# Another order of the units in a grouped-query attention, and the wait of its output projection

## The chip, the cores and the metric

The kernel runs on one core of a Trainium2 chip. The metric is the device time of one execution in microseconds; the kernel before was timed three times (median 2070.47, from 2069.06 to 2070.81). The engines are PE (TensorE), DVE (VectorE), ACT (ScalarE), POOL (GpSimd) and SP (which here only issues transfers); each works through its own instructions in order, and they wait for each other by semaphores.

## What is computed

The whole reference is a chain: a first block (differential attention, neighbourhood attention, a mixture of experts, a gated side input) and then two layers over 512 tokens and a context of 256 rows, all in float32 with a model width of 1024. The first of these two layers holds the grouped-query attention that the change touches. Its 16 query heads of 64 columns share 4 key and value heads. Queries of the 512 tokens see 768 keys (256 of the context, 512 of the tokens); queries of the context see only the context's 256 keys. Both results are gated and go through the same output projection:

```
o  = gqa_attend(q,  concat(kc, k), concat(vc, v))     # 512 rows, 768 keys
y  = (o * silu(g)) @ w_out
qc = rms_norm(proj_c[..., q columns])
oc = gqa_attend(qc, kc, vc)                           # 256 rows, 256 keys
yc = (oc * silu(gc)) @ w_out
```

`gqa_attend` is scores times head_dim ** -0.5, a softmax in float32 and the product with the values. `y` and `yc`, scaled by a gate, are added to the residual, and the second of the two layers (a latent attention, MLA) starts from a norm of that.

## The kernel before, in words

Rows are worked on in tiles of 128: tiles 0 to 3 are the tokens, 4 and 5 the context (`XT` = 4, `AT` = 6). Everything here stands in `second_layers` (L1607); both attentions of this part of the kernel are made by the class `Attention` (L233), which writes out the instruction streams of PE (`tensor`, L294), DVE (`vector`, L429), ACT (`scalar`, L499) and POOL (`gpsimd`, L418).

The work of the grouped-query attention is a list of units, built in L1763. A unit is one pair of heads `p` (eight pairs) and one query tile `t`: for `t` of 0 to 3 over all six key tiles (a token unit), for `t` of 4 and 5 over key tiles 4 and 5 (a context unit). Six units make a pair, four for tokens and then two for the context, so there are 48. The fifth entry of a unit is its output group: the token units of pair `p` are group `2p`, its context units group `2p + 1`. `out_of` (L1767) says where a group's result goes: `gT_x[:, p]` for the tokens, `gT_c[:, p]` for the context, both preloaded with silu of the gate.

For each unit PE makes the scores of both heads into four PSUM banks (L324; there is one such area, so the scores of unit n+1 wait until the exponentials of unit n have read it), DVE finds the negated row maxima (L440), and ACT makes the exponentials with their row sums (L515). PE transposes the weights in pieces of four tiles (L336: three pieces for a token unit, one for a context unit), and the pieces are copied to SBUF by ACT (the first of a unit) and DVE (the others), both through the helper line L205. PE then multiplies them with the values (L350). When the last unit of a group is through, DVE takes the reciprocals of the sums (L496), POOL spreads them over the head's columns (L427), PE transposes them (L370), and DVE multiplies gate, sum and reciprocal in two steps (L472, L477).

PE's order in step n is written out in L379 to L393: scores of unit n+1; the turn, if one is due; the weights of unit n; the values of unit n-1; and the reciprocals' transposes if unit n-1 closed a group. DVE's order (L482 to L497) is: the maxima of unit n+1, its pieces of the turn, its pieces of the weights of unit n, and the closing. ACT's (L521 to L527) is: its pieces of the turn, its piece of the weights, the exponentials of unit n+1.

A turn is the transposition of the next pair's queries (and, for pairs 0, 2, 4 and 6, of the next key head) from rows to columns (`gqa_turn`, L1750; PE in L309). It has two pieces of 4 and 2 tiles for the queries and, on an even pair, two more of 4 and 2 tiles for the keys, which are copied twice. The first and third piece are DVE's, the second and fourth ACT's. A turn is due two steps before the first unit of its pair (`turn_step`, L250), that is in the step of the fifth unit of the pair before. Turn pieces, weight pieces and reciprocals go through one ring of three PSUM banks: a piece is written when the piece three before it has been emptied (`take`, L298 to L303).

Behind the attention PE starts the output projection (L1908 to L1943): for both context tiles and both halves of the output columns, four products of eight matmuls of 512 columns each (L1847), whose first seven steps need the groups of pairs 0 to 6 and whose last needs pair 7. Then follow the tokens' tiles, and the norm and the products of the next layer in an order written out in `low_order` (L1684). SP issues the next layer's first weights once the last value product is counted (L1801). The projection adds its result to the residual in L2242 and L2244.

Of the kernel before, what the change touches and what calls it, by code (L numbers as in the profile page):

```python
# [19 lines left out]
DK = D // P  # L20
GRID_W, ROWS, CB = 64, 8, 16
SEQ, CTX = 512, 256
XT, CT = SEQ // P, CTX // P
AT = XT + CT
# [182 lines left out]
def view(t, at, *dims):  # L207

    v = t[:, at:at + math.prod(dims)]
    if len(dims) == 1:  # L210
        return v
    axes = "abcd"[:len(dims)]
    return v.rearrange(f"p ({' '.join(axes)}) -> p {' '.join(axes)}", **dict(zip(axes, dims)))
# [19 lines left out]
class Attention:  # L233
# [56 lines left out]
    def slot(self, n):  # L290
        og = self.units[n][4]
        return og % 2, n - self.members[og][0]
# [1314 lines left out]
def second_layers(nc, c, m, A, base, side_w, extra, arena, ring_in, mods, tabs_2, l1_tabs, ys):  # L1607
# [4 lines left out]
    TT = (4, 5, 0, 1, 2, 3)  # L1612
    at6 = XT * D + CT * D + XT * 96 + XT * 32 + 2 * AT * 32 + 64
    (tc, tsn, tk, _), ((gain_0, shift_0, gate_0), (gain_1, shift_1, gate_1)) = l1_tabs, mods


# [4 lines left out]
    gT_x, gT_c = view(arena, 21504, DK, SEQ), view(arena, 25600, DK, CTX)  # L1621
# [128 lines left out]
    def gqa_turn(p):  # L1750
        q_of = [proj[:, t, 512 + p * P:512 + (p + 1) * P] for t in range(AT)]
        k_of = [proj[:, t, (p // 2) * 64:(p // 2 + 1) * 64] for t in range(AT)]
        pieces = [(q_of[a:e], P, [qT[:, p % 2, a * P:e * P]]) for a, e in ((0, 4), (4, AT))]
        if p % 2 == 0:
            pieces += [(k_of[a:e], 64, [kT[64 * x:64 * x + 64, p // 2 % 2, a * P:e * P] for x in range(2)]) for a, e in ((0, 4), (4, AT))]
        return pieces

    def gqa_ready(pe):
        pe.wait_ge(s["normed"], 18)
        pe.wait_ge(s["ev_act"], units.by[unit["g", DK - 1]][1] + 1)  # L1760
    gqa = Attention(nc, m, sem_of("gqa_"), dict(S=S, T=T, O=O, pr=view(arena, 27648, 2, 2, AT * P), pT=view(arena, 8192, 2, 2 * AT, P), nm=nm, sm=sm, rc=rc, ratio=None,
                                                wide=view(side_w, 3072, 2, 4, 2, 64)),
                    [(p, t, 0, AT, 2 * p, t) if t < XT else (p, t, XT, AT, 2 * p + 1, t - XT) for p in range(8) for t in range(AT)], 2, 1,  # L1763
                    [gqa_turn(p) for p in range(8)],
                    2, lambda p, x, t, lo, hi: (qT[64 * x:64 * x + 64, p % 2, t * P:(t + 1) * P], kT[64 * x:64 * x + 64, p // 2 % 2, lo * P:hi * P]),
                    lambda p, x, kt: proj[:, kt, 256 + (p // 2) * 64:256 + (p // 2 + 1) * 64], 64,
                    lambda og: gT_c[:, og // 2] if og % 2 else gT_x[:, og // 2], gate=True, ready=dict(ring=gqa_ready))  # L1767

    q1T, k1T = view(arena, 8192, 2, 2, SEQ), view(side_w, 0, 2, 2, AT * P)

# [21 lines left out]
    with nc.Block() as block:  # L1792
# [39 lines left out]
        def _(pe):  # L1832
            done = [0]

            def start(key):

                u = unit[key]
                assert u == done[0], key
                done[0] += 1
                if u >= 4:  # L1840
                    act, k = units.by[u - 4]
                    pe.wait_ge(s["ev_act"] if act else s["ev_dve"], k + 1)
                return ps[:, u % 4]

            def product(out, lhs, rhs, ks, K=DK):
                for k in ks:
                    last = pe.matmul(out, lhs(k), rhs(k), start=(k == 0), stop=(k == K - 1))  # L1847
                return last
# [9 lines left out]
            weights_of = lambda i: (lambda k: slot(i + k // 4)[:, k % 4])  # L1858
# [53 lines left out]
            gated = lambda t: (lambda k: gT_x[:, k, t * P:(t + 1) * P]) if t < XT else (lambda k: gT_c[:, k, (t - XT) * P:(t - XT + 1) * P])  # L1912
            first = {(t, cc): start(("o", t, cc)) for t in (4, 5) for cc in range(2)}
            for (t, cc), out in first.items():
                product(out, gated(t), weights_of(2 * cc), range(DK - 1))
            pe.wait_ge(s["gqa_emptied_act"], gqa.emptied[1])
            pe.wait_ge(s["gqa_emptied_dve"], gqa.emptied[0])
            for (t, cc), out in first.items():
                product(out, gated(t), weights_of(2 * cc), (DK - 1,)).then_inc(s["mm"], 1)
            seen_norms = 0  # L1920
            arrived_1 = lambda i, n: pe.wait_ge(s["weights_in"][i], 16 * n)
            for what, t in low_order[2:]:
# [38 lines left out]
            first = {(t, cc): start(("z", t, cc)) for t in (0, 1) for cc in range(2)}  # L1961
# [428 lines left out]
def build(nc, A, prm_at, const_at, stop=None, dbg=None):  # L2390
    with ExitStack() as top:
        def sb(c, name, shape, dt=F32):
            return c.enter_context(nc.sbuf_tensor(name, shape, dt))

        prm = sb(top, "params", [P, sum(n for _, n in prm_at.values())])
        cst = sb(top, "consts", [P, sum(n for _, n in const_at.values())])
        m = {k: prm[:, a:a + n] for k, (a, n) in prm_at.items()}
        m.update({k: cst[:, a:a + n] for k, (a, n) in const_at.items()})


        words = [XT * D, CT * D, XT * 96, XT * 32, 2 * AT * 32, 64, 4 * AT * 64, AT * DK, AT * DK, 2 * D, AT * DK, AT * DK, D]
        base = sb(top, "residual", [P, sum(words)])
        at = lambda n: sum(words[:n])
        hx = view(base, 0, AT, D)
        tc, tsn, tk = view(base, at(2), XT, 96), view(base, at(3), XT, 32), view(base, at(4), 2, AT, 32)
        tkn, tabs_2 = view(base, at(5), 1, 64), view(base, at(6), 4, AT, 64)
        mods = [[view(base, at(7), AT, DK), view(base, at(8), AT, DK), view(base, at(9), 2, D)],
                [view(base, at(10), AT, DK), view(base, at(11), AT, DK), view(base, at(12), 1, D)]]
        rows = lambda v: v.rearrange("(t p) d -> p t d", p=P)

        side_w = sb(top, "side", [P, XT * D])
        extra, arena = sb(top, "extra", [P, 2112]), sb(top, "arena", [P, 30720])
        with semaphores(nc, "ahead", ring_in=6) as ahead:
            with ExitStack() as c:
                ys = first_layer(nc, c, m, A, prm, cst, const_at, base, side_w, extra, arena, ahead["ring_in"], mods, tabs_2, (tc, tsn, tk, tkn))
            with ExitStack() as c:
                second_layers(nc, c, m, A, base, side_w, extra, arena, ahead["ring_in"], mods, tabs_2, (tc, tsn, tk, tkn), ys)
# [34 lines left out]
```

## Time and profile before

| | |
|---|---|
| median of 3 runs | 2070.47 us (2069.06 to 2070.81) |
| the profiled execution: its time, its span | 2071.58 us, 2069.8 us |
| mean granted TensorE clock | 0.958 of full speed |
| PE busy | 1811.1 us, 88% of the span |
| PE weight loads | 1016.0 us, 49% |
| DVE busy | 734.1 us, 35% |
| ACT busy | 521.6 us, 25% |
| POOL busy | 150.3 us, 7% |
| chain that ended last, by engine | PE 31%, issue 17%, DVE 2%, ACT 2%, POOL 1% |

Times in the rows are counted from the span's start. "Busy" is a share of the span. In a timeline a row is a run of like instructions: start, length, engine, line, operation, output and inputs, how many, and in brackets how long the engine had been idle before it and what it had waited for. Matmuls are pipelined, so that the length of a row of them reaches a little into the next one; the distance of two starts is what counts. The grouped-query attention runs from 1262 to 1487 us, the latent attention from 1782 on. The granted clock (PEclk) is the share of full speed that the chip's throttle gave TensorE in a stretch: 1.00 is 2.4 GHz, and the lower level is half of it.

### The profile page before, as it was taken

The page shows a single profiled execution, that of the slowest core. Times are in us where ns is not written, and L with a number is a line of the kernel's source. Part 1 is how long each engine was busy: PE and PEld are TensorE (multiplying, and loading weights), DVE is VectorE, ACT ScalarE, POOL GpSimd, SP SyncE. Part 2 cuts the span into 40 slices and gives each one's busy share as a digit, 9 for nine tenths or more (in the row PEclk, how much of TensorE's full clock was granted, in tenths as well). Part 3 has the DMA queues.
Part 4 walks back from the last instruction along what each step waited for, and adds up shares of the span by engine and source line. Part 5 has one row for each costly group of instructions (what it writes and reads, how often), then busy time and mean ns, then how long its engine had stood idle before and what let it go on. Part 6 is the DMA issues. An engine that isn't in the chain of part 4 may idle for free.

```text
span 2069.8 us, 24033 instructions
## 1 busy us (share of the span) xinstructions
PE 1811.1 (88%) x9628; PEld 1016.0 (49%) x9628; DVE 734.1 (35%) x1431; ACT 521.6 (25%) x1102; POOL 150.3 (7%) x201
## 2 busy tenths in 40 slices
PE   7999878978887778784999998888998999699998
PEld 3333455544444444442464444666644544466663
DVE  2333576231131110120213264666424225455542
ACT  2111476210000001110223123444311233234330
POOL 1110000001111111100000130000000000100000
PEclk9999899999999999997999999999999999899999
DMA  7554937369999999996432220000200011000001
GB/s 246 205 195 166 182 54 119 115 264 387 420 420 420 421 420 421 418 421 262 176 109 81 81 81 1 1 1 2 90 6 31 21 56 61 21 1 1 1 22 41
DMA packets 91871, 333.18 MB, mean 161 GB/s; under 512 B 10096, under 2 KB 26608, under 8 KB 64752
## 3 DMA queue, kind: packets, MB, share of 16 engines
q1 hardware_dynamic: 81536, 310.56, 41.2%
q0 software_dynamic: 5120, 16.78, 2.0%
q10 hardware_dynamic: 5104, 4.30, 0.7%
q8 instruction: 77, 1.26, 0.3%
q14 instruction: 34, 0.28, 0.0%
HBM read 317.32 MB, written 14.30 MB: 160 GB/s over the span
## 4 chain that ended last, share of the span: by engine, by line
PE 31%; issue 17%; DVE 2%; ACT 2%; POOL 1%; POOLq 0%; ACTq 0%; DVEq 0%
PE tail_ps L1847 27%; PE tail_ps L324 2%; ACT arena L515 1%; PE tail_ps L1855 1%; PE tail_ps L336 1%; POOL side L427 1%; POOL extra L2384 1%; PE tail_ps L350 0%; DVE arena L2343 0%; PE tail_ps L309 0%; DVE side L205 0%; DVE tail_small L440 0%; DVE arena L2344 0%; PE tail_ps L370 0%; DVE residual L2244 0%
## 5 line engine op out<-in xcount | busy, mean ns | idle before, releaser
L987 PE MATMUL mix_ps<-arena 128*64 128x256 f32 x2048 | 258.9, 410 | 88.9 <-issue 60.3
L987 PEld LDWEIGHTS mix_ps<-arena 128*64 128x64 f32 x2048 | 165.4, 148 | 181.6 <-issue 90.2
L1847 PE MATMUL tail_ps<-arena 128*128 128x512 f32 x504 | 219.7, 592 | 0.0
L440 DVE TENSOR_REDUCE tail_small<-tail_ps 128x1 f32<-128x768 f32 (+1 forms) x160 | 128.7, 846 | 156.6 <-PE tail_ps L324 156.6
L875 PE MATMUL mix_ps<-arena,side 128*128 128x512 f32 x384 | 174.2, 607 | 9.8 <-DVE side L1201 9.8
L1847 PEld LDWEIGHTS tail_ps<-arena 128*128 128x128 f32 x504 | 95.1, 190 | 115.0 <-issue 114.3
L515 ACT ACTIVATE arena<-tail_ps,tail_small 128x768 f32<-128x768 f32 (+1 forms) x160 | 128.6, 813 | 5.9 <-DVE tail_small L440 5.9
L875 PEld LDWEIGHTS mix_ps<-arena,side 128*128 128x128 f32 x384 | 72.3, 193 | 111.1 <-issue 83.8
L1847 PE MATMUL tail_ps<-arena,side 128*128 128x512 f32 (+2 forms) x320 | 122.7, 545 | 0.0
L999 PE MATMUL mix_ps<-arena 128*64 128x512 f32 x512 | 116.9, 598 | 2.2 <-issue 1.6
L336 PE MATMUL tail_ps<-consts,arena 128*128 128x128 f32 x832 | 110.8, 283 | 1.0 <-ACT arena L515 0.2
L336 PEld LDWEIGHTS tail_ps<-consts,arena 128*128 128x128 f32 x832 | 95.6, 145 | 20.5 <-issue 17.3
L324 PE MATMUL tail_ps<-side,arena 96*128 96x512 f32 (+1 forms) x256 | 94.3, 513 | 8.7 <-ACT arena L515 8.1
L1382 DVE COPY arena<-mix_ps 128x256 f32<-128x256 f32 x31 | 13.2, 425 | 224.4 <-PE mix_ps L992 224.0
L1847 PEld LDWEIGHTS tail_ps<-arena,side 128*128 128x128 f32 x320 | 62.6, 197 | 57.4 <-issue 45.4
L1154 ACT ACTIVATE arena<-mix_ps,mix_small 128x512 f32<-128x512 f32 x31 | 21.3, 687 | 269.6 <-PE mix_ps L999 269.6
L324 PE MATMUL tail_ps<-side 64*128 64x256 f32 (+1 forms) x320 | 65.0, 519 | 21.7 <-ACT arena L515 20.6
L1847 PE MATMUL tail_ps<-side,arena 128*128 128x512 f32 x192 | 83.9, 592 | 0.0
L324 PEld LDWEIGHTS tail_ps<-side,arena 96*128 96x128 f32 x256 | 47.8, 197 | 49.4 <-issue 35.7
L999 PEld LDWEIGHTS mix_ps<-arena 128*64 128x64 f32 x512 | 34.4, 136 | 60.6 <-issue 57.1
L1847 PE MATMUL tail_ps<-arena,extra 128*128 128x512 f32 (+1 forms) x128 | 51.4, 562 | 12.4 <-PEq L161 12.4
L1555 POOL DMA_INDIRECT expert_out<-arena,mix_indices x31 | 30.7, 989 | 424.3 <-ACT arena L1154 417.6
(343 smaller groups left out, 2182.1 us busy)
## 6 DMA issues: line engine op xcount, KB each, us to landing
arena<-in_w SPq DMA_DIRECT2D x96, 2048.0 KB, 18.1
arena<-in_l_w_in SPq DMA_DIRECT2D x22, 1024.0 KB, 7.4
arena<-in_l_w_mod SPq DMA_DIRECT2D x16, 1024.0 KB, 5.0
arena<-in_w_in SPq DMA_DIRECT2D x12, 1024.0 KB, 9.9
arena<-in_l_w_mod SPq DMA_DIRECT2D x16, 512.0 KB, 4.6
residual<-bias_blocks SPq DMA_DIRECT2D x32, 224.0 KB, 11.1
arena<-in_l_w_out SPq DMA_DIRECT2D x6, 1024.0 KB, 5.2
arena<-in_w_out SPq DMA_DIRECT2D x4, 1024.0 KB, 13.3
```

The source lines that it names most:

```text
L324: ins = pe.matmul(self.scores_of(n, x)[:, a * P:e * P], q, k, start=True, stop=True)
L336: ins = pe.transpose(Tp[:, bank, z * P:(z + 1) * P], pr[:, n % self.PRB, x, kt * P:(kt + 1) * P], m["ident"])
L427: pool.tensor_copy(wide[:, og % 2, 0:k], rc[:, og % 2, 0:k, 0:heads].unsqueeze(3).to_broadcast([P, k, heads, P // heads])).then_inc(s["spr ...
L440: dve.tensor_reduce(nm[:, b, x:x + 1], self.scores_of(n, x), AX.X, ALU.max, negate=True).then_inc(s["maxed"], 1)
L515: act.activation(pr[:, b, x, 0:k], in_, ACT.Exp, bias=nm[:, b, x:x + 1], scale=scale, accum_out=sm[:, og_b, z, x:x + 1]).then_inc(s["exped ...
L875: last = pe.matmul(ps[:, u % 4], oT[:, k, t * P:(t + 1) * P], weights.slot(W_IN[n, k // 4], 4, 512)[:, k % 4], start=(k == 0), stop=(k == ...
L987: last = pe.matmul(out[h * CAP:(h + 1) * CAP, 0:H2], x, wb[:, k, h * H2:(h + 1) * H2], start=(k == 0), stop=(k == DK - 1))
L999: last = pe.matmul(py[h * CAP:(h + 1) * CAP, :], x, wb[:, f, h * 512:(h + 1) * 512], start=(f == 0), stop=(f == FK - 1))
L1154: act.activation(yb[:, e % 2], py, ACT.Copy, scale=gate_w[:, e:e + 1]).then_inc(s["y_out"], 1)
L1555: pool.indirect_dma_start(out=y_rows, out_offset=bass.IndirectOffsetOnAxis(ap=index[:, 1, e:e + 1], axis=0), in_=yb[:, e % 2], in_offset=N ...
L1847: last = pe.matmul(out, lhs(k), rhs(k), start=(k == 0), stop=(k == K - 1))
L1855: last = pe.transpose(ps[:, pair(key) + k // 4, k % 4 * P:(k % 4 + 1) * P], src(k), m["ident"])
```

## The change

The two context units of each pair come first, then its four token units. The group numbers change with them: the context units of pair `p` are now group `2p`, its token units `2p + 1`. The four first products of the output projection, which are the context's, wait with their last step for the closing of the last context group (`gqa.ogs - 2`) alone; the waits for everything that the attention empties now stand behind these products, ahead of token tile 0.

```
@@ second_layers: the list of units
-   [(p, t, 0, AT, 2 * p, t) if t < XT else (p, t, XT, AT, 2 * p + 1, t - XT) for p in range(8) for t in range(AT)], 2, 1,
+   [(p, t, 0, AT, 2 * p + 1, t) if t < XT else (p, t, XT, AT, 2 * p, t - XT) for p in range(8) for t in TT], 2, 1,
...
-   lambda og: gT_c[:, og // 2] if og % 2 else gT_x[:, og // 2], gate=True, ready=dict(ring=gqa_ready))
+   lambda og: gT_x[:, og // 2] if og % 2 else gT_c[:, og // 2], gate=True, ready=dict(ring=gqa_ready))
@@ second_layers, tensor: the output projection
        for (t, cc), out in first.items():
            product(out, gated(t), weights_of(2 * cc), range(DK - 1))
+       pe.wait_ge(s["gqa_emptied_dve"], gqa.closed(gqa.ogs - 2))
+       for (t, cc), out in first.items():
+           product(out, gated(t), weights_of(2 * cc), (DK - 1,)).then_inc(s["mm"], 1)
        pe.wait_ge(s["gqa_emptied_act"], gqa.emptied[1])
        pe.wait_ge(s["gqa_emptied_dve"], gqa.emptied[0])
-       for (t, cc), out in first.items():
-           product(out, gated(t), weights_of(2 * cc), (DK - 1,)).then_inc(s["mm"], 1)
```

`TT` is (4, 5, 0, 1, 2, 3). The wait ahead of the first 28 matmuls, `gqa.closed(gqa.ogs - 3)`, is unchanged in its text; group 13 was the context of pair 6 and is now its tokens. The step in which a turn is due is still that of the fifth unit of a pair.

## Rows read from the trace of the kernel before

**Rows 1.** Busy time by stretch: us, then each engine, PEclk, DMA share, GB/s
```profile
1328.50:1356.62 28.12, 24.76 (x221) 17.53 (x220) 16.58 (x27) 12.85 (x31) 1.02 (x2) 0.94 0.00 1
1356.62:1384.84 28.22, 24.05 (x228) 17.31 (x227) 17.95 (x29) 13.61 (x33) 1.02 (x2) 1.00 0.00 1
1384.84:1411.94 27.10, 23.12 (x222) 16.63 (x221) 16.57 (x27) 12.85 (x31) 1.02 (x2) 1.00 0.01 2
1469.00:1487.45 18.45, 17.84 (x187) 13.38 (x187) 11.10 (x20) 8.34 (x21) 1.02 (x2) 1.00 0.00 1
```

**Rows 2.** Waits within the attention: us in total, times, longest us
```profile
PE tail_ps L324 <- ACT arena L515: 20.6, 24, 2.9
...
PE tail_ps L370 <- POOL side L427: 8.8, 7, 1.7
```

**Rows 3.** Timeline of PE, one period with an odd turn
```profile
1389.50 1.56 PE L324 MATMUL tail_ps<-side 64*128 64x512 f32 x8 [0.18 <-ACT arena L515]
1390.99 1.53 PE L336 MATMUL tail_ps<-consts,arena 128*128 128x128 f32 x12
1392.45 1.53 PE L350 MATMUL tail_ps<-arena 128*64 128x128 f32 x24
1394.16 0.70 PE L324 MATMUL tail_ps<-side 64*128 64x256 f32 x4 [0.18 <-ACT arena L515]
...
1397.71 0.70 PE L324 MATMUL tail_ps<-side 64*128 64x256 f32 x4
1398.35 0.88 PE L309 MATMUL tail_ps<-consts,arena 128*128 128x128 f32 x6
...
1401.63 1.56 PE L324 MATMUL tail_ps<-side 64*128 64x512 f32 x8
...
1406.30 1.56 PE L324 MATMUL tail_ps<-side 64*128 64x512 f32 x8 [1.93 <-ACT arena L515]
...
1411.60 0.41 PE L370 MATMUL tail_ps<-consts,side 128*128 128x128 f32 x2 [1.70 <-POOL side L427]
```

**Rows 4.** Timeline of PE, an even turn in a context unit
```profile
1314.48 0.41 PE L309 MATMUL tail_ps<-consts,arena 128*64 128x128 f32 x2 [0.20 <-DVE side L205]
```

**Rows 5.** Timeline of PE, scores at the start
```profile
1261.97 1.56 PE L324 MATMUL tail_ps<-side 64*128 64x512 f32 x8 [0.95 <-DVE side L205]
...
1271.05 1.56 PE L324 MATMUL tail_ps<-side 64*128 64x512 f32 x8 [1.58 <-ACT arena L515]
...
1280.31 0.70 PE L324 MATMUL tail_ps<-side 64*128 64x256 f32 x4 [0.18 <-ACT arena L515]
```

**Rows 6.** Timeline of PE, the end of the attention and the projection
```profile
1486.49 0.66 PE L350 MATMUL tail_ps<-arena 128*64 128x128 f32 x8 [0.25 <-ACT arena L205]
...
1487.45 41.44 PE L1847 MATMUL tail_ps<-arena 128*128 128x512 f32 x96
```

**Rows 7.** Timeline of DVE
```profile
1272.64 1.82 DVE L440 TENSOR_REDUCE tail_small<-tail_ps 128x1 f32<-128x768 f32 x2 [1.58 <-PE tail_ps L324]
1274.38 1.28 DVE L205 COPY arena<-tail_ps 128x512 f32<-128x512 f32 x2
...
1281.04 0.76 DVE L440 TENSOR_REDUCE tail_small<-tail_ps 128x1 f32<-128x256 f32 x2 [0.78 <-PE tail_ps L324]
...
1313.74 1.97 DVE L205 COPY side<-tail_ps 128x512 f32<-128x512 f32 x3
...
1487.76 0.42 DVE L477 TENSOR_TENSOR arena<-arena,tail_ps 128x256 f32<-128x256 f32 x1
```

**Rows 8.** Timeline of ACT
```profile
1273.73 0.90 ACT L515 ACTIVATE arena<-tail_ps,tail_small 128x768 f32<-128x768 f32 x1
...
1282.64 0.47 ACT L515 ACTIVATE arena<-tail_ps,tail_small 128x256 f32<-128x256 f32 x1
```

**Rows 9.** Timeline of PE, the latent attention's turn in a full unit
```profile
1808.02 1.30 PE L309 MATMUL tail_ps<-consts,arena 128*96 128x128 f32 x10 [0.98 <-DVE arena L205]
```

**Rows 10.** Busy time by stretch, all behind the attention
```profile
1487.45:2069.80 582.35, 532.99 (x2455) 313.10 (x2454) 236.69 (x383) 156.71 (x303) 17.01 (x28) 0.97 0.09 31
```

## The prediction

> **What bounds the kernel now.** The page's shares come first: PE (TensorE) is busy 88% of the span and carries most of the chain that ended last, so what PE waits for, and how long its own work lasts, is time. The change touches only the grouped-query attention and the seam to its output projection, so the next view is the busy time by stretch, cut where PE starts the third token scores of each pair. PE stands for 225.5 us between its first scores there (1261.97) and the first projection matmul (1487.45) [rows 5, 6]: 9.08 us to the first cut, seven periods, 18.45 us after the last cut. A period is 27.10 us when the next pair needs only queries turned (odd pairs, four times) and 28.22 when keys too (even, three times), at a granted clock of 1.00; five of the seven ran at 0.94 and took about 1 us more, as 28.12 against 27.10 shows [rows 1]. The waits name two releasers: scores wait for ScalarE's exponentials, 20.6 us in all, and the transposes of the spread reciprocals wait for GpSimd, 8.8 us [rows 2].
>
> PE's timeline of one period shows where. A token unit is 1.49 us of scores, 1.46 of twelve transposes, 1.46 of 24 value matmuls, then 0.18 of waiting: 4.66 us, PE and the chain scores, maximum, exponential nearly level. Two places are open: the second token scores (1406.30) wait 1.93 us, since only two context units' short work covers the exponential of the first, and the context's reciprocal transposes (1411.60) wait 1.70 us for GpSimd [rows 3]. The end of the attention, which the change is about, is closed already: PE waits 0.25 us once and then runs 96 projection matmuls with no idle time [rows 6].
>
> **The change, part by part.**
>
> *The moved wait.* Today the context's last head pair closes last and 4 of the 32 first matmuls are held behind its closing; afterwards all 32 wait only for a group that closed six units before. VectorE's last multiply for the attention starts 0.31 us after the projection starts and takes 0.42 us, while PE does the first 28 matmuls of 0.43 us, 12 us [rows 6, 7]. So the wait is never met: worth 0. Behind the new wait stand PE's products for token tile 0; the last group's multiply, 0.69 instead of 0.42, is then hidden by 32 matmuls, 13.8 us. SP's loads for the next layer go out on the last value product, which stays just ahead of the projection: 0. The same instructions are issued, only in another order; GpSimd's sixteen copies too: 0.
>
> *The end.* From the last cut to the projection it is 18.45 us now [rows 1]. Afterwards two token units end the list: 4.66 to the last scores; from there 4.66 until its exponentials are done; then 1.46 of transposes, 1.46 and 1.46 of values (the first covers the copies of the last transposes, the second GpSimd's spread), 0.5 for four reciprocal transposes: 14.2 us. **-4.2 us.**
>
> *The start.* It is 9.08 us to the first cut now, with two token units issued [rows 5]. Afterwards two context units come before them. Scores to scores for a context unit with nothing else to do: VectorE's maxima start 0.73 after PE (1280.31, 1281.04) and take 0.38 each; an engine starts 0.18 after what it waits for (768 columns: 0.91 of maximum, exponential after 1.09, 1272.64 to 1273.73); then two exponentials of 256, of 0.47 and overlapping a little, and 0.18 to PE: 2.4 us [rows 5, 7, 8]. For the second one the copy of a transposed piece stands ahead on ScalarE; its second exponential starts 2.33 after the scores (1280.31, 1282.64) [rows 5, 8]; with 0.47 and 0.18 that is 3.0 to the first token scores. Then 4.66 with the 1.93 wait in it, and 5.65 with GpSimd's (1406.30 to 1411.94) [rows 1, 3]: 15.7 us. **+6.6 us.** This is the eighth passage from context to tokens; before there are seven, since there none precedes pair 0.
>
> *The turn of the next pair's queries and keys.* It stays at the fifth unit of a pair, and that was the first context unit and is now the third token unit. This is the largest term. Removed from the context unit: an odd turn takes 0.73 us of PE there (six transposes of 0.12) [rows 3]; an even one 1.12 more [rows 1], so 1.85. What is left between the second context scores and the next token scores, 3.92 (1397.71 to 1401.63) less 0.73, is 3.2 us of PE, above the 3.0 of the exponentials [rows 3]. Added to the token unit: PE hands over through a ring of three PSUM banks, and VectorE empties a turn's first piece only behind the two maxima of 768 columns of the scores just made. Those end late: with scores at T the maxima start at T+1.59 and the next copy at T+3.33 (1271.05, 1272.64, 1274.38) [rows 5, 7], and PE goes on 0.74 after such a copy begins (1313.74, 1314.48) [rows 4, 7]: T+4.07. An odd turn is two pieces, the weights' first piece takes the third bank, and its second must wait for that T+4.07, where PE would be ready at T+2.7. Then eight transposes 0.97 and values 1.46: next scores at T+6.50 instead of T+4.66, +1.84. Per odd turn +1.84-0.73=+1.11. An even turn is four pieces: the fourth waits until T+4.07, ends at 4.31, the weights' first at 4.80; their second waits for VectorE's third copy (0.65 each, start T+4.63, +0.74): 5.37, then 0.97 and 1.46: T+7.80, +3.14. Per even turn +3.14-1.85=+1.29. Four and three of them: **+8.3 us.** The exponentials come in time in both: for odd turns at T+4.66 and the 0.73 by which ScalarE gets its first weights later, for even ones behind its copies of the fourth piece, at about T+7.7. The other attention has a turn in a full unit today, and there PE waits 0.98 us in mid turn for exactly such a copy [rows 9]: this stall is real, not only deduced. Bounds: below, if VectorE's order did not matter, PE's work and ScalarE's delayed exponentials alone give T+5.4 and about T+6.2, that is 0 per odd and -0.3 per even turn, -0.9 in all; above, an extra fall of the clock with each.
>
> *The clock.* Five of seven passages are followed by a stretch at 0.94, at about 1 us each. I take the eighth at 5/7 of that: **+0.7 us.**
>
> Sum: -4.2+6.6+8.3+0.7=+11.4 us. The profiled execution took 2071.58 (span 2069.8), 1.1 above the median of 2070.47; so 2083.0 beside it, and 2081.9 against the median.
>
> The clock is where a rule speaks against the change. The rows show that PE keeps its higher level of 2.4 GHz through two periods that have the same waits as the five that lose it (28.22 and 27.10 at 1.00, 28.12 at 0.94) [rows 1]: waits of 1 to 2 us are sometimes punished and sometimes not. The Trainium skill ("TensorE: Matmul & The Clock Gate", section "A second HAM failure mode: psum-queue depth-cycling") says that small idle times between groups, from cycling through PSUM banks, can by themselves make the clock go back and forth between its two levels. By that rule the new ring stalls would each cost a fall as well; that is the first rival below.
>
> **The rivals.**
>
> *More clock falls.* Place: the seven token units with a turn, now with 1.4 us of idle PE, and all eight passages. Price: fifteen falls for five, ten more at 1 us; in place of my 0.7: 10.7+10=+21 us, 2091. For it: five of seven passages had one. Against it: two had none with the same waits, and a stall of 1.4 us is shorter than the 1.93 before those falls. Chance 0.16, mostly as a part of it (2086 to 2091).
>
> *The turn costs nothing.* If pieces were emptied early enough, the turns give -0.9 in place of +8.3: -4.2+6.6-0.9+0.7=+2.2, 2072.7, within the noise. Against it stand [rows 4, 9], where PE waits for this copy. This includes the case that the change does little: the wait it moves is already hidden, and the order of units only rotated. Chance 0.12.
>
> *Faster, by the clock.* Place: the five slow stretches here and, downstream, the rest of the kernel at a mean of 0.97 over 582 us [rows 10], some 17 us of lost clock. If another spacing of the waits kept TensorE at 2.4 GHz, it would give 5 us here and up to 17 later, against my +10.7 without falls: -11, as low as 2059. It makes the kernel faster once it gives back over 15 us, so most of it. The stage after is unchanged, so there is little for it. Chance 0.05.
>
> **How the numbers follow.** My forecast, with 2078 to 2086 as its own range (turns between half and a fifth more than reckoned, clock by two falls either way), has 0.67. About 0.2% (4.1 us) is what a measurement of this kernel can tell from no change. Faster 0.05; same 0.12, the hidden turns; slower 0.83, the forecast and the first rival. The range for eight in ten leaves out most of the hidden turns, the faster case and the very end of the clock rival: 2074 to 2090.
>
> **What would show it.** In PE's timeline: the third token unit with the turn takes 6.5 (odd) or 7.8 us (even) to the next scores, with about 1.4 us of idle time released by VectorE's copies into the turned queries; the second context scores to the next token scores 3.2 us; the first two token scores of pair 0 start some 5.3 us later than now; the projection starts 14.2 us after the last third-token scores, again without idle time. First scores to projection: 236 to 237 us for 225.5. I am wrong if those waits are missing, or if a wait stands at the projection's start in the kernel before that these rows don't show, or if the periods at 0.94 become twice as many or vanish.

## The result, and the profile after

The changed kernel is slower: 2088.91 us median of 4 runs (2084.78 to 2094.26) against 2070.64 of 4 (2069.06 to 2072.0), a ratio of 1.0081 with a 95% interval of 1.0061 to 1.0100. Timed again with more runs beside it: 2088.79 of 6 against 2073.22 of 21, 1.0079 (1.0060 to 1.0097), that is +16 us, between 12 and 20. The forecast was 2081.9 in a range of 2074 to 2090.

The profiled execution took 2084.78 us, 13.2 more than the one of before. Ahead of the attention it is 2.6 us longer, in the attention 13.8 longer, and behind it 3.1 shorter; the stretches ahead and behind are taken up with the last four profiles. The busy time by stretch in the kernel after, cut at the first scores and at the first projection matmul (us, then busy time of PE, weight loads, DVE, ACT, POOL, then PEclk, DMA share, GB/s):

```profile
0.00:1264.53 1264.53, 1082.90 (x5403) 562.76 (x5403) 361.42 (x829) 258.89 (x546) 124.89 (x157) 0.96 0.69 249
1264.53:1503.77 239.24, 198.25 (x1773) 140.93 (x1774) 136.07 (x220) 105.97 (x254) 8.10 (x16) 0.95 0.00 1
1503.77:2083.00 579.23, 529.69 (x2456) 310.54 (x2454) 237.07 (x383) 156.68 (x303) 16.98 (x28) 0.97 0.09 31
```

The attention takes 239.2 us where it took 225.5 (1261.97 to 1487.45 in [rows 5, 6]): +13.8. The matmuls are the same. PE is busy for 198.3 us there, 3.2 more than before, and idle for 41.0, 10.6 more: most of what is new is waiting. The waits of PE in that stretch of the kernel after (us in total, times, longest):

```profile
PE tail_ps L324 <- ACT arena L515: 20.0, 18, 1.9
PE tail_ps L370 <- POOL side L427: 10.6, 8, 1.7
PE tail_ps L336 <- DVE side L205: 6.4, 7, 1.3
PE tail_ps L309 <- DVE side L205: 3.8, 3, 1.3
```

The first two lines answer to [rows 2]: hardly changed, though GpSimd is waited for eight times and not seven. The last two are VectorE's copies out of the turn. The kernel before had such waits only in its three even turns, 0.20 us each as in [rows 4]; now there are ten, 10.2 us. PE's timeline of an odd turn, on to the next tokens' first scores, is shown next. A step is measured from one unit's scores to the next unit's. PE makes scores one unit ahead, so the step of the third token unit begins with the scores of the fourth:

```profile
1347.44 1.56 PE L324 MATMUL tail_ps<-side 64*128 64x512 f32 x8 [0.18 <-ACT arena L515]
1348.93 0.87 PE L309 MATMUL tail_ps<-consts,arena 128*128 128x128 f32 x6
1349.64 0.60 PE L336 MATMUL tail_ps<-consts,arena 128*128 128x128 f32 x4
1351.51 1.09 PE L336 MATMUL tail_ps<-consts,arena 128*128 128x128 f32 x8 [1.26 <-DVE side L205]
1352.53 1.53 PE L350 MATMUL tail_ps<-arena 128*64 128x128 f32 x24
1353.99 0.70 PE L324 MATMUL tail_ps<-side 64*128 64x256 f32 x4
...
1357.54 0.70 PE L324 MATMUL tail_ps<-side 64*128 64x256 f32 x4
...
1360.81 1.56 PE L324 MATMUL tail_ps<-side 64*128 64x512 f32 x8
```

VectorE in the same stretch:

```profile
1349.03 1.82 DVE L440 TENSOR_REDUCE tail_small<-tail_ps 128x1 f32<-128x768 f32 x2 [1.64 <-PE tail_ps L324]
1350.77 0.68 DVE L205 COPY side<-tail_ps 128x512 f32<-128x512 f32 x1
```

With T=1347.44 the maxima start at T+1.59, the copy of the turn's first piece at T+3.33, and PE goes on at T+4.07. The next scores come at T+6.55 (forecast 6.50) where they came at T+4.66 in [rows 3], and the passage from the second context scores to the tokens is 3.27 us (1357.54 to 1360.81) where it was 3.92. An even turn holds PE twice:

```profile
1376.60 1.56 PE L324 MATMUL tail_ps<-side 64*128 64x512 f32 x8 [0.18 <-ACT arena L515]
1378.09 1.31 PE L309 MATMUL tail_ps<-consts,arena 128*128 128x128 f32 x10
1380.67 0.41 PE L309 MATMUL tail_ps<-consts,arena 128*64 128x128 f32 x2 [1.26 <-DVE side L205]
1380.91 0.60 PE L336 MATMUL tail_ps<-consts,arena 128*128 128x128 f32 x4
1381.95 1.09 PE L336 MATMUL tail_ps<-consts,arena 128*128 128x128 f32 x8 [0.44 <-DVE side L205]
1382.97 1.53 PE L350 MATMUL tail_ps<-arena 128*64 128x128 f32 x24
1384.43 0.70 PE L324 MATMUL tail_ps<-side 64*128 64x256 f32 x4
```

That is 7.83 us (forecast 7.80). The two ends of the attention, again PE's timeline:

```profile
1264.53 0.70 PE L324 MATMUL tail_ps<-side 64*128 64x256 f32 x4 [0.95 <-DVE side L205]
1266.77 0.70 PE L324 MATMUL tail_ps<-side 64*128 64x256 f32 x4 [1.54 <-ACT arena L515]
...
1270.04 2.93 PE L324 MATMUL tail_ps<-side 64*128 64x512 f32 x8 [1.60 <-ACT arena L515]
...
1276.46 1.56 PE L324 MATMUL tail_ps<-side 64*128 64x512 f32 x8 [1.68 <-ACT arena L515]
...
1282.10 1.56 PE L324 MATMUL tail_ps<-side 64*128 64x512 f32 x8
```
```profile
1489.72 1.56 PE L324 MATMUL tail_ps<-side 64*128 64x512 f32 x8
...
1494.38 1.56 PE L324 MATMUL tail_ps<-side 64*128 64x512 f32 x8 [0.18 <-ACT arena L515]
...
1503.77 6.60 PE L1847 MATMUL tail_ps<-arena 128*128 128x512 f32 x15
```

From first scores to the third token scores it is 17.57 us for 9.08: +8.5, where +6.6 was forecast. One step accounts for the miss: from the first token scores to the second it is 6.42 us (1270.04 to 1276.46) where 4.66 was reckoned, and its scores 2.93 for 1.56, at TensorE's lower clock. From the last third-token scores to the projection it is 14.05 for 18.45: -4.4 (forecast -4.2).

The account of the 13.8 us: start +8.5, end -4.4, four odd turns at 6.55-4.66-(3.92-3.27)=+1.24 and three even ones at 7.83-4.66-(5.03-3.27)=+1.41, together +9.2; 0.5 remain: 0.3 in one step of 4.94, where the scores wait 0.46 us for the exponentials and not 0.18, and 0.2 for the clock. Of the seven passages after the first, three ran free of the lower clock (two of seven before).

### The profile page after: what moved, and what is told of

It is laid out like the page before. It is cut to its first block, busy times and chain, and to the rows that moved or that the text cites. A ratio compares the mean times of both kernels' runs of the same rounds, so it can differ in the third digit from the quotient of the medians.

```text
span 2083.0 us, 24037 instructions
## 1 busy us (share of the span) xinstructions
PE 1810.8 (87%) x9628; PEld 1014.2 (49%) x9628; DVE 734.6 (35%) x1431; ACT 521.5 (25%) x1102; POOL 150.0 (7%) x201
## 3 DMA queue, kind: packets, MB, share of 16 engines
q8 instruction: 77, 1.26, 0.3%
## 4 chain that ended last, share of the span: by engine, by line
PE 30%; issue 18%; DVE 2%; ACT 1%; POOL 1%; POOLq 0%; ACTq 0%; DVEq 0%
PE tail_ps L1847 26%; PE tail_ps L324 2%; ACT arena L515 1%; PE tail_ps L1855 1%; PE tail_ps L336 1%; POOL side L427 1%; POOL extra L2385 1%; DVE arena L2344 0%; PE tail_ps L309 0%; PE tail_ps L350 0%; DVE side L205 0%; DVE arena L2345 0%; PE tail_ps L370 0%; DVE residual L2245 0%; DVE arena L2243 0%
## 5 line engine op out<-in xcount | busy, mean ns | idle before, releaser
L1382 DVE COPY arena<-mix_ps 128x256 f32<-128x256 f32 x31 | 13.2, 425 | 221.3 <-PE mix_ps L992 219.0
L205 ACT ACTIVATE arena<-tail_ps 128x512 f32<-128x512 f32 (+1 forms) x56 | 33.5, 597 | 116.9 <-PE tail_ps L336 107.0
```

Source lines behind the costliest of these rows:

```text
L205: return eng.activation(out, in_, ACT.Copy) if act else eng.tensor_copy(out, in_)
```

## The experiments

All but the four profiled executions at the end were timed beside the kernel before, in two batches: four with a median of 2073.22 for it, the other four with 2073.43. A ratio is to the kernel before of the same batch.

**The changed kernel again.** No edit.

> The changed kernel, unchanged, once more. Its profiled execution (span 2083.0) was the shortest of its four times (2084.8 to 2094.3), so what the attention shows, +13.8 us, is less than the medians differ by, +18.3. Theory A (the order of units and the place of the turn set the time, the rest is the clock's luck): the stretch from first scores to projection again takes 237 to 242 us, the turns 6.5 and 7.8 us, and what varies between executions is the granted clock and the expert stage in code that the change leaves alone; median between 2082 and 2090. Rival C (the new stalls cost more clock than the first profile shows): the stretch takes over 244 us, with ten or more slow stretches in it, and the median is 2088 or above.

Ratio 1.0079; the attention took 238.3 us, the turns 6.55 and 7.84. Rival C falls here as far as one profile goes, though this one, too, is of the shortest of its six timed executions; the last four profiles come back to it.

**The change with the turn back in a context unit.** The new argument, whose default leaves everything as it was, is given to the grouped-query attention alone.

```
-        self.turn_step = {self.first_of[g] - LEAD - 1: g for g in range(1, self.groups)}
+        self.turn_step = {self.first_of[g] - (ahead(g) if ahead else LEAD + 1): g for g in range(1, self.groups)}
...
+   gate=True, ready=dict(ring=gqa_ready), ahead=lambda g: 6)
```

> The changed kernel with the turn of the next pair six steps ahead of its first unit and not two: in the step of the first context unit, where it stood in the kernel before. Theory A (VectorE empties a turn's piece only behind two 768-column maxima): the third token unit falls from 6.55 and 7.83 us back to 4.66, the passage from the second context scores to the tokens grows from 3.27 back to 3.9 and 5.0; -8.3 us, less 0.7 for the first turn, which now stands in the first context unit of all; first scores to projection 231.6 us, and 7.6 us under the changed kernel timed beside it. Rival B (it is the context units in front that cost, wherever the turn stands): no more than 2 us under the changed kernel.

Measured: 2075.83 us median, ratio 1.0012 (1.0000 to 1.0024) where the changed kernel beside it had 1.0079: 0.67%, 14 us less. In the profile the attention takes 229.5 us for 238.3, -8.8, the third token unit 4.75 us, the passages with an odd and an even turn 3.92 and 4.98. PE's waits in the attention:

```profile
PE tail_ps L324 <- ACT arena L515: 19.7, 17, 1.9
PE tail_ps L370 <- POOL side L427: 11.5, 8, 1.7
PE tail_ps L324 <- DVE arena L205: 1.9, 7, 0.3
PE tail_ps L324 <- DVE side L205: 0.9, 1, 0.9
PE tail_ps L309 <- DVE side L205: 0.6, 3, 0.2
```

The 10.2 us behind VectorE's copies are down to 0.6, three times the 0.20 of [rows 4]; 1.9 us of waits for copies of the weights are new, 0.3 each. Rival B is out. The times differ by 13 to 14 us and the stretch by less: 8.8, or 10 against the mean of four profiles of the changed kernel. The rest is not placed.

**The old order with the turn in a full unit.** The same edit on the kernel before, with `ahead=lambda g: 4`.

> The kernel before, its order of units kept, but with the turn four steps ahead of the pair's first unit: in the step of the third token unit, as the change has it. Theory A: +1.1 us for each of four odd turns and +1.3 for each of three even ones, +8.3 us; first scores to projection 233.8 us for 225.5; 2078.8 for 2070.5. Rival B: within 2 us of the kernel before, since the order of units is the old one.

Measured: 1.0038 (1.0021 to 1.0056), +7.9 us. The same waits appear in an order of units that is otherwise the old one:

```profile
PE tail_ps L370 <- POOL side L427: 8.8, 7, 1.7
PE tail_ps L336 <- DVE side L205: 6.4, 7, 1.3
PE tail_ps L309 <- DVE side L205: 3.8, 3, 1.3
```

The attention took 236.4 us. By its steps 9.2 of the +10.9 are the turns (6.55 and 7.84, passages 3.27); the rest is the lower clock, six steps that lost 6.7 us where five lost 5.0. The profiled execution was the longest of the ten, which spread widely (2074.6 to 2093.2, at mean granted clocks from 0.965 down to 0.953), so that here the steps say more than the ratio. The largest term needs nothing of the change but the step in which the turn falls.

**The change with the old waits at the projection.**

```
             for (t, cc), out in first.items():
                 product(out, gated(t), weights_of(2 * cc), range(DK - 1))
-            pe.wait_ge(s["gqa_emptied_dve"], gqa.closed(gqa.ogs - 2))
-            for (t, cc), out in first.items():
-                product(out, gated(t), weights_of(2 * cc), (DK - 1,)).then_inc(s["mm"], 1)
             pe.wait_ge(s["gqa_emptied_act"], gqa.emptied[1])
             pe.wait_ge(s["gqa_emptied_dve"], gqa.emptied[0])
+            for (t, cc), out in first.items():
+                product(out, gated(t), weights_of(2 * cc), (DK - 1,)).then_inc(s["mm"], 1)
```

> The changed kernel with the old waits at the projection: the last step of the first four products waits for everything that the attention empties. Theory A: the wait is hidden by 28 matmuls of 0.43 us, 12 us, against VectorE's two multiplies of 0.7 us, so no idle time appears in the projection and the time is that of the changed kernel timed beside it, within 1 us but for the clock. Rival D (the moved wait is worth something in this order, where the token group closes last): 1 to 3 us slower, with idle time ahead of the 29th matmul.

Measured: 2088.21 us, 1.0066 (1.0048 to 1.0083), no slower than the change (1.0079), as far as intervals of this width tell. PE and VectorE around the projection's start:

```profile
1505.77 0.66 PE L370 MATMUL tail_ps<-consts,side 128*128 128x128 f32 x4
1506.26 24.20 PE L1847 MATMUL tail_ps<-arena 128*128 128x512 f32 x56
```
```profile
1505.88 0.69 DVE L472 TENSOR_TENSOR arena<-tail_ps,arena 128x512 f32<-128x512 f32 x1 [1.75 <-PE tail_ps L350]
1506.72 0.69 DVE L477 TENSOR_TENSOR arena<-arena,tail_ps 128x512 f32<-128x512 f32 x1
```

VectorE's last multiply ends at 1507.4, 1.2 us into the projection; the 29th matmul, which now waits for it, comes 12 us in, and there is no gap. As a wait of PE the moved wait is worth nothing in either place. Rival D falls.

**The change with ScalarE emptying the whole turn.** `turn_act` is true for the grouped-query attention alone.

```
-            self.place(("turn", 0, j), j % 2)
+            self.place(("turn", 0, j), 1 if turn_act else j % 2)
...
-                    self.place(("turn", self.turn_step[n], j), j % 2)
+                    self.place(("turn", self.turn_step[n], j), 1 if turn_act else j % 2)
```

> The changed kernel with all pieces of a turn in the grouped-query attention emptied by ScalarE, so that no piece of a turn stands behind VectorE's maxima; the turn stays in the third token unit. Theory A (PE is held there by VectorE's order): the wait for VectorE's copy disappears; the step is then bound by ScalarE's own order (turn copies, weights copy, exponentials): about 5.5 us for 6.55 in the odd turns and 7.5 for 7.83 in the even ones, -5.2 us, less about 1 at the first turn, where two engines shared the copies: 4 us under the changed kernel. Rival B (the longer step is only the turn's own work): no change, or slower by ScalarE's added copies.

Measured: 1.0039 (1.0023 to 1.0055), 8 us under the change. PE's timeline of an odd turn:

```profile
1345.83 1.56 PE L324 MATMUL tail_ps<-side 64*128 64x512 f32 x8 [0.18 <-ACT arena L515]
1347.32 0.87 PE L309 MATMUL tail_ps<-consts,arena 128*128 128x128 f32 x6
1348.03 1.73 PE L336 MATMUL tail_ps<-consts,arena 128*128 128x128 f32 x12
1349.68 1.53 PE L350 MATMUL tail_ps<-arena 128*64 128x128 f32 x24
1351.28 0.70 PE L324 MATMUL tail_ps<-side 64*128 64x256 f32 x4
```

No wait is left inside this step, which takes 5.45 us (expected 5.5) and so is PE's own work. In the odd turns it is the order of VectorE's work that held PE, and not the turn as such. The even ones fall only from 7.84 to 7.46 (7.5): ScalarE's copies and the exponentials behind them now hold PE, by 0.36 us in mid turn and 0.36 ahead of the next scores. The attention took 234.0 us, -4.3 against the changed kernel's second profile and about as expected; the times fell by 8, of which the stretch explains half.

**The second wait of the passage: the kernel before with the reciprocal at the head of its step.** The passage from context to tokens costs two waits in [rows 3]. The spread comes late since VectorE takes the reciprocals last in its step; the sums they need are complete a step earlier. VectorE and GpSimd in the kernel before, at the passage of [rows 3] that ends at 1411.60:

```profile
1410.82 0.17 DVE L496 RECIPROCAL tail_small<-tail_small 128x4 f32<-128x4 f32 x1
```
```profile
1411.05 0.40 POOL L427 COPY side<-tail_small 128x256 f32<-128x256 f32 x1 [10.46 <-DVE tail_small L496]
```

The edit:

```
         for n in range(N + 1):
+            if n - 1 in self.closes and self.rows_to is None:
+                og = self.closes[n - 1]
+                k = len(self.members[og])
+                dve.wait_ge(s["exped"], n * L)
+                dve.reciprocal(rc[:, og % 2, 0:k, :], sm[:, og % 2, 0:k, :]).then_inc(s["inverted"], 1)
             if self.combine is not None and n < N:
...
-                if self.rows_to is None:
-                    dve.wait_ge(s["exped"], n * L)
-                    dve.reciprocal(rc[:, og % 2, 0:k, :], sm[:, og % 2, 0:k, :]).then_inc(s["inverted"], 1)
```

> The kernel before with VectorE's reciprocal of a closed group at the head of its step, ahead of the maxima and the copies, in both attentions. Theory A (the passage from context to tokens costs two waits, 1.93 for the exponentials and 1.70 for GpSimd's spread, and the second is late because the reciprocal stands last on VectorE): the 1.70 disappears, the step falls from 5.64 to 4.66 us at full clock; -6.9 us for seven of them, and about -5 in the latent attention, where PE waits 0.78 us at a closing: 12 us under the kernel before, near 2061. Rival (the spread is slow for GpSimd's own reasons, or the passage is bound by the exponentials alone): under 2 us.

Measured: 2062.01 us, 0.9941 (0.9926 to 0.9955), -12.2 us. A passage in PE's timeline:

```profile
1301.36 1.56 PE L324 MATMUL tail_ps<-side 64*128 64x512 f32 x8 [1.92 <-ACT arena L515]
...
1304.90 0.44 PE L370 MATMUL tail_ps<-consts,side 128*128 128x128 f32 x2
1306.02 1.56 PE L324 MATMUL tail_ps<-side 64*128 64x512 f32 x8 [0.68 <-ACT arena L515]
```

The 1.70 us are gone, 0.68 of them come back as a wait for the exponentials, and the step takes 4.66 for 5.64. The attention took 217.9 us. The latent attention, from first scores to its projection, took 218.5 for 226.6 us, with no wait for GpSimd left (5.5 us before); another 2.3 us of the difference are its first two steps, which PE ran at more of the lower clock in the kernel before.

**Both repairs on the changed order.** The turn six steps ahead and the early reciprocal, as above.

> The changed kernel's order with both repairs: the turn in the first context unit, the reciprocal at the head of its step. Its stretch from first scores to projection was 229.5 us with the first repair; eight passages at 0.98 us less give 221.7, about 3 us above the kernel before with the same second repair (218.6), since the order has an eighth passage (+6.6, or +8.4 as measured) and a shorter end (-4.4). If the context-first order had a gain of its own, it would now be level or below.

Measured: 2064.93 us, 0.9956 (0.9941 to 0.9971), against 0.9941 for the old order with one repair: the attention 223.0 us (expected 221.7) against 217.9. Of the 5.1 us between the two, 2.7 are the lower clock (five such steps against three) and some 2.3 the order. Context first has no gain of its own to set against its eighth passage. Since the intervals overlap, this rests on one profile of each.

**A version that beats both.** Context units last in even pairs and first in odd ones.

```
-   [... for p in range(8) for t in TT]
+   [(p, t, 0, AT, 2 * p + p % 2, t) if t < XT else (p, t, XT, AT, 2 * p + 1 - p % 2, t - XT)
+    for p in range(8) for t in (TT if p % 2 else range(AT))]
...
-   lambda og: gT_x[:, og // 2] if og % 2 else gT_c[:, og // 2]
+   lambda og: gT_x[:, og // 2] if og % 2 == og // 2 % 2 else gT_c[:, og // 2]
+   gate=True, ready=dict(ring=gqa_ready), ahead=lambda g: 2 if g % 2 else 6)
```

The edit is against the changed kernel, and the early reciprocal comes with it.

> A candidate to beat both: the context units stand last in even pairs and first in odd ones, so that four of them follow each other and only four passages from context to tokens remain; the attention starts and ends with token units; every turn stands in a context unit; the reciprocal stands at the head of its step. Theory A: a block of two pairs takes 53.1 us (seven token steps of 4.66, one of 4.91, context steps of 3.6, 3.9, 3.0 and 5.1), first scores to projection 214.6 us and up to 2 for the clock; -5 in the latent attention: 15 us under the kernel before, near 2058. Rival B (context units in front cost as such): not below the kernel before with the early reciprocal.

Measured: 2057.37 us (2054.91 to 2057.89), 0.9915 (0.9900 to 0.9931), -17.6 us against the kernel before, and its interval lies under the changed order with both repairs. The attention takes 217.6 us, 3 more than reckoned. A block of two pairs is 3.56, 3.92, 2.95 and 4.94 us for the context steps, but the third token unit of an odd pair takes 4.75, and two steps ran at the lower clock (6.26 and 6.29 for 4.66). In the profiles its attention is level with that of the old order and its early reciprocal (217.9, with three such steps), and 3.8 us of the 4.3 between the two spans (2060.4 and 2056.1) stand ahead of the attention, in code that they share. So it beats both kernels of this case, but that it beats the early reciprocal alone is not shown: the two intervals overlap.

**Four more profiled executions**, two of either kernel.

> The kernel before, another profiled execution. The medians differ by some 16 us, the attention in the profiles by 13 to 14. If the clock's phase is all that varies, the attention takes 220.5 us plus about 1 us for each slow stretch, four to eight of them (the first profile had five: 225.5); if the first profile was a lucky one, over 228. What comes ahead of the attention (1262.0 us in the first) varies by up to 10 us whatever the kernel.

> The changed kernel, another profiled execution: first scores to projection 237 to 242 us with five to eight slow stretches (rival C: over 244, ten or more, in an execution that is longer than those profiled so far); the turns at 6.5 and 7.8 us as before.

> As the first look at the kernel before: 224 to 229 us from first scores to projection, and a start of the attention anywhere from 1260 to 1273 us.

> As the first look at the changed kernel: 237 to 242 us from first scores to projection, and a start of the attention anywhere from 1260 to 1273 us, like that of the kernel before; if it starts later than the kernel before does, the rest of the difference of the medians stands there.

The attention in these, the kernel before first:

```profile
1269.30:1494.64 225.34, 195.03 (x1772) 139.56 (x1773) 136.11 (x220) 105.85 (x254) 8.10 (x16) 0.96 0.01 1
```
```profile
1269.49:1496.57 227.08, 196.05 (x1772) 139.75 (x1773) 136.10 (x220) 106.00 (x254) 8.15 (x16) 0.95 0.00 1
```
```profile
1263.11:1501.49 238.38, 196.64 (x1772) 139.29 (x1773) 135.76 (x220) 105.99 (x254) 8.14 (x16) 0.96 0.00 1
```
```profile
1268.10:1510.51 242.41, 201.36 (x1772) 141.66 (x1773) 135.87 (x220) 105.84 (x254) 8.10 (x16) 0.94 0.00 1
```

Three profiles of the kernel before give 225.5, 225.3 and 227.1 us, each with five steps at the lower clock; four of the changed one give 239.2, 238.3, 238.4 and 242.4, with six, five, five and eight. The means are 226.0 and 239.6: +13.6. So rival C is not what happens as a rule, but its mechanism can be seen in the last of them.

Outside the attention the profiles vary too. Its start lies between 1262.0 and 1269.5 us before and between 1263.1 and 1268.1 after, behind code that neither kernel changes. From the projection's first matmul to the end, the kernel before took 582.4, 582.4 and 579.9 us, the changed one 578.6 to 579.2, some 2.6 less. This is TensorE's clock again: in all of these profiles, and in that of the changed kernel with the old waits, PE starts the same work at the same distance, within 0.1 us, up to 113 us behind the projection's first matmul, and in the 50 us that begin 100 us behind it the granted clock was 0.83 or 0.93 before and 0.86 or 0.93 after. The changed kernel with the old waits took 582.3 us there; whether the moved wait has a hand in where the clock falls so much later is not shown.

On the mean the whole spans of the profiles differ by 9.3 us (2083.7 and 2074.4), the timed executions by 16, and the difference is not placed. By chance both timed profiles of the changed kernel fell on the shortest execution of their batch, and its ten timed executions had a mean granted clock of 0.957, the kernel before 0.960 in the 39 beside the experiments. More time at the lower clock is the likely rest, but no profile shows where.

## Why the prediction was right or wrong

**The moved wait, 0**: right; with the old waits put back PE still has no gap in the projection. (The last steps of the first four products wait for a group that closes four units before the end, and not six as the prediction has it; it makes no difference.) **The end, -4.2**: -4.4. **The turns, +8.3**: +9.2 by the steps of the profile. The token unit's side was right to 0.05 us. The small error is on the other side: I took 3.2 us for what stays of the passage and subtracted 0.73 and 1.85, and it is 3.27, so 0.65 and 1.76 were freed. That the turn's place makes them is shown from both sides: the turn moved in the old order brings the waits, the turn moved back takes them away. That it is VectorE's order is shown for the odd turns, where emptying by ScalarE leaves no wait; in the even ones it puts ScalarE's order in its place.

**The start, +6.6**: mis-sized; +8.5. The two context steps came to 2.24 and 3.27 (2.4 and 3.0 reckoned), and the error is in the step that I took at 4.66 us: it ran at 6.42, and at 6.42 to 6.43 in all four profiles of the changed kernel. In the old order the step from the second to the third token scores ran at 4.60 in two profiles and at 6.42 in the third (6.43 in the one with the turn moved), so the same thing can happen there, but less often. Why the changed start loses the clock each time stays open. **The clock, +0.7**: I put it at the passage, where I counted one eighth fall of 1 us; it came in the step ahead of the passage and cost 1.8.

Of the rivals, "the turn costs nothing" and "faster, by the clock" are out. "More clock falls" asked for fifteen; there were five to eight. The seven ring stalls of 1.26 us per execution brought a fall in one of the 28 turns of the four profiles (the first has a step of 9.45 for 7.84). The Trainium skill ("TensorE: Matmul & The Clock Gate", section "A second HAM failure mode: psum-queue depth-cycling") tells of a kernel in which frequent small idle times between groups of matmuls make the clock oscillate. That each stall costs a fall was the prediction's strong reading of it, and the measurement goes against that reading; that the clock goes back and forth in such a stretch it bears out, with five to eight falls, though not that the ring is what brings them.

The forecast of 2081.9 was low by 7 us: 2088.9 lies inside the wide range, near its upper end, and outside the forecast's own range of 2078 to 2086. Against the +16 us of the larger timing the +11.4 was low by 5. In the attention it was low by 2.4 of 13.8 in the first profile, and all four profiles (238.3 to 242.4) lie above the 236 to 237 foretold; what is left between 13.6 and 16 stands in no profile. The direction, the order of the terms and the place of each wait were as told; the fall of the clock at the start was not.

## What to carry to other kernels

A step of setup work that stands at a fixed distance ahead of its group moves when the group's units are put in another order; look at which step it lands in, and at what each engine does first there. A reciprocal, a sum or another small result that is ready a step early belongs at the head of the engine's step and not behind its long work: here that gave 12 us, where the reordering took 16. And before a wait is moved, look at whether anybody waits there: here the trace had 96 matmuls without a gap behind it.

## What was not expected of the hardware

TensorE's lower clock (half speed) followed short waits by no fixed rule: after an idle time of 1.93 us the same step took 5.64 us in two of seven passages of the kernel before and 6.39 to 7.01 in the other five, and its third profile had five slow steps again, in part other ones. And a single profiled execution says little of a few per mille: the start of the attention lay between 1262.0 and 1272.8 us over the ten profiles of kernels that have the same instructions ahead of it.
